# Modulation and first norm in one stage, and the mixing product begun inside the recurrence

## The reference

```
# first block, start
mod = silu(c) @ w_ada + b_ada                       # w_ada 1024 x 6144
sh_m, sc_m, g_m, sh_f, sc_f, g_f = split(mod, 6)
h = rms_norm(x, norm_mix) * (1 + sc_m) + sh_m
y = fox_mixer(h, ...)                               # begins with h @ w_in (q, k, v and 16 forget gates)
...
# second block
pool_out = multiscale_pool(...)
rwkv_out = rwkv7_mix(...)                           # a recurrence over tokens, 12 heads of 64
mixed = concatenate([pool_out, rwkv_out]) @ w_out   # 1024 x 1024
h = layer_norm(DEEPNORM_ALPHA * x + mixed, ln1_g, ln1_b)
ffn = hierarchical_moe(h, ...)                      # router logits, two of 32 experts per token
```

## Time and profile before

| | |
|---|---|
| median of 3 runs | 3073.77 us (3071.57 to 3078.01) |
| time of the profiled execution | 3072.45 us |
| its span in the profile | 3070.6 us |
| TensorE busy | 2856.3 us, 93% of the span |
| VectorE, ScalarE, GpSimd busy | 50%, 24%, 9% |
| granted TensorE clock, mean | 0.984 of full |

### The profile page before, as it was taken

One profiled execution on the slowest core, in us unless ns is written; L12 is line 12 of the kernel. 1 busy time (PEld: TensorE's weight loads), 2 busy tenths in 40 slices (PEclk: granted clock), 3 DMA queues, 4 the chain that ended last, 5 costly groups with the idle time before them and its releaser, 6 DMA issues. The chain is left out here.

```text
span 3070.6 us, 52396 instructions
## 1 busy us (share of the span) xinstructions
PE 2856.3 (93%) x20752; PEld 1903.6 (62%) x20752; DVE 1535.7 (50%) x4101; ACT 724.2 (24%) x1655; POOL 261.9 (9%) x343
## 2 busy tenths in 40 slices
PE   3999989989999999999999999999999797999996
PEld 2787456664688545885445777777777554444442
DVE  4543056761455566655654566666666366011115
ACT  2211056551200000000003344343444200111111
POOL 0000011100000000000000222121222100101001
PEclk9999999999999999999999999999999897999998
DMA  5101023321023453224453000000000200999965
GB/s 202 47 28 55 0 98 103 110 78 41 28 83 110 153 176 123 93 106 154 169 187 132 17 11 25 3 25 25 2 25 3 101 35 21 347 350 357 350 249 192
DMA packets 103873, 338.88 MB, mean 110 GB/s; under 512 B 6864, under 2 KB 16592, under 8 KB 94560
## 3 DMA queue, kind: packets, MB, share of 16 engines
q1 hardware_dynamic: 95696, 306.35, 27.9%
q0 software_dynamic: 6912, 25.17, 2.2%
q10 hardware_dynamic: 1040, 4.19, 0.3%
HBM read 302.60 MB, written 33.10 MB: 109 GB/s over the span
## 5 line engine op out<-in xcount | busy, mean ns | idle before, releaser
L1840 PE MATMUL rwkv_ps<-all_main,pre_ws 128*128 128x256 f32 x1152 | 290.9, 389 | 0.0
L1183 PE MATMUL mlp_ps<-mlp_w2s,all_main 128*128 128x512 f32 x512 | 239.6, 592 | 0.0
L2761 PE MATMUL ex_pg<-all_main,ex_xT 128*128 128x512 f32 x512 | 225.5, 594 | 0.0
L1840 PEld LDWEIGHTS rwkv_ps<-all_main,pre_ws 128*128 128x128 f32 x1152 | 207.6, 190 | 28.9
L2207 DVE TENSOR_TENSOR all_tail<-rwkv_ps,all_tail 128x256 f32<-128x256 f32 x216 | 91.6, 424 | 191.4 <-PE rwkv_ps L1946 144.7
L1183 PE MATMUL mlp_ps<-all_main 128*128 128x512 f32 x384 | 183.2, 592 | 0.7 <-DVE all_main L1396 0.7
L2761 PEld LDWEIGHTS ex_pg<-all_main,ex_xT 128*128 128x128 f32 x512 | 97.6, 191 | 122.4 <-issue 122.4
L1183 PEld LDWEIGHTS mlp_ps<-mlp_w2s,all_main 128*128 128x128 f32 x512 | 96.6, 190 | 117.8 <-issue 105.4
L2151 POOL TENSOR_TENSOR all_tail<-all_tail,pre_cst 128x256 f32<-128x256 f32 x120 | 99.9, 847 | 472.9 <-DVE all_tail L2207 299.3
L2068 ACT COPY all_tail<-rwkv_ps 128x256 f32<-128x256 f32 (+1 forms) x216 | 83.0, 396 | 219.4 <-PE rwkv_ps L1937 184.2
L1183 PEld LDWEIGHTS mlp_ps<-all_main 128*128 128x128 f32 x384 | 72.7, 190 | 93.2 <-issue 69.4
(11 more groups left out here) (439 smaller groups left out, 5087.9 us busy)
## 6 DMA issues: line engine op xcount, KB each, us to landing
mlp_w2s<-in_w SPq DMA_DIRECT2D x64, 1024.0 KB, 4.9
all_main<-in_w_gu SPq DMA_DIRECT2D x32, 2048.0 KB, 9.8
all_early<-in_w SPq DMA_DIRECT2D x32, 1024.0 KB, 4.7
att_wa<-in_w_ada SPq DMA_DIRECT2D x32, 512.0 KB, 3.9
all_early<-in_w_d SPq DMA_DIRECT2D x16, 1024.0 KB, 11.7
all_main<-in_w_d SPq DMA_DIRECT2D x16, 1024.0 KB, 11.2
y_rows<-ex_y SPq DMA_DIRECT2D x32, 512.0 KB, 3.1
qkv_wq<-in_w_qkv SPq DMA_DIRECT2D x6, 2048.0 KB, 7.5
```

The source lines that it names most:

```text
L1183: last = nc.tensor.matmul(ps[:, PRODUCTS.index(name), :], lhsT=lhsT, rhs=rhs, start=j == 0, stop=j == FPAIRS - 1)
L1840: last = nc.tensor.matmul(ps[:, bank, 0:UT], lhsT=ws[:, n, k, :], rhs=xT[:, k, (col + NB) % S:(col + NB) % S + UT], start=(k == 0), stop=( ...
L2761: last = nc.tensor.matmul(pg[:, n % 2, :], lhsT=xT[:, n % 2, k, :], rhs=gu[n][:, k, :], start=(k == 0), stop=(k == KT - 1))
```

## The change

`stage_modulation` and `stage_norm` become one block, `stage_start`. SP issues all its loads without a wait: first `x` in two halves of 2 MB, then `w_ada` in eight pieces of 1 MB, each into a place of its own in `main`. ScalarE squares a half and also scales it (an ACTIVATE in place of VectorE's multiplication). VectorE's accumulator is cut in two parts of 1024 columns, and TensorE waits for each apart; VectorE's two small steps for the second token half stand behind k = 1 and k = 2 in its list. TensorE transposes seven rounds into seven banks before it sums the columns, and the other nine after. The sixteen rounds are taken alternately by ScalarE and VectorE.

In the second block the PSUM tensor is now opened ahead of both stages. The layer norm's rows are loaded at the end of the recurrence's SP list. TensorE computes token tile 0 of the mixing product inside `stage_rwkv`, eight matmuls ahead of its last `body` and eight behind it; in `stage_mix_route` it starts with tile 1 and has no wait for `c_in` until the first logits.

```diff
-def stage_modulation(nc, x, cols1, w_ada, xres, modc, cols, silu, ones):
...
+def stage_start(nc, x, cols1, w_ada, xres, main, modc, cols, silu, hT, ones, ident):
...
+        pt = s.ps("pt", [P, 7, NB])
...
+        acc = main[:, 0:2, 2 * D:3 * D]
...
+        def bank(r):
+            return r % 7
+
+        def wait_taken(eng, r):
+
+            eng.wait_ge(taken_v if r % 2 else taken_a, r // 2 + 1)
...
                 sp.dma_start(cols[:], cols1).then_inc(cols_in, 16)
-                for g in range(KT // 2):
-                    if g >= 2:
-                        sp.wait_ge(w_used, 2 * g - 2)
-                    sp.dma_start(wa[:, g % 2, :, :], w_ada[2 * g * P:(2 * g + 2) * P, 0:2 * D].rearrange("(k p) c -> p k c", p=P)
-                                 ).then_inc(w_in[g % 2], 16)
+                for half in range(2):
+                    sp.dma_start(xres[:, half_of(half), :], x[half * NB:(half + 1) * NB, :].rearrange("(t p) d -> p t d", p=P)
+                                 ).then_inc(x_in[half], 16)
+                for k in range(KT):
+                    sp.dma_start(main[:, k, 0:2 * D], w_ada[k * P:(k + 1) * P, 0:2 * D]).then_inc(w_in[k], 16)
 
             @block.scalar
             def _(act):
                 act.wait_ge(cols_in, 16)
                 nc.scalar.activation(work[:, 0, :], cols[:, 0:KT], ACT.Exp, scale=-1.0).then_inc(silu_exp, 1)
-                act.wait_ge(w_in[1], 16)
-                act.dma_start(xres[:], x.rearrange("(t p) d -> p t d", p=P)).then_inc(x_in, 16)
-                act.wait_ge(x_in, 16)
+                for half in range(2):
+                    act.wait_ge(x_in[half], 16)
+                    for t in range(half * HT, (half + 1) * HT):
+                        nc.scalar.activation(xn[:, t, :], xres[:, t, :], ACT.Square, accum_out=ss[:, t:t + 1]).then_inc(sq_done, 1)
+                    act.wait_ge(var_ok, half + 1)
+                    nc.scalar.activation(st[:, 1, half_of(half)], st[:, 0, half_of(half)], ACT.Sqrt).then_inc(root, 1)
+                    act.wait_ge(rstd_ok, half + 1)
+                    for t in range(half * HT, (half + 1) * HT):
+                        nc.scalar.activation(xn[:, t, :], xres[:, t, :], ACT.Identity, scale=st[:, 2, t:t + 1]).then_inc(xn_done, 1)
+                act.wait_ge(finished, 3)
+                for r in range(0, 2 * KT, 2):
+                    half, c = r // KT, r % KT
+                    act.wait_ge(turned, r + 1)
+                    nc.scalar.activation(hT[:, c, half * NB:(half + 1) * NB], pt[:, bank(r), :], ACT.Identity,
+                                         scale=modc[:, 0, 0, c:c + 1], bias=modc[:, 0, 1, c:c + 1]).then_inc(taken_a, 1)
+                act.wait_ge(taken_a, KT)
...
+                def variance(half):
+                    dve.wait_ge(sq_done, (half + 1) * HT)
+                    nc.vector.tensor_scalar(st[:, 0, half_of(half)], ss[:, half_of(half)], 1.0 / D, EPS, ALU.mult, ALU.add
+                                            ).then_inc(var_ok, 1)
+
+                def inverse_root(half):
+                    dve.wait_ge(root, half + 1)
+                    nc.vector.reciprocal(st[:, 2, half_of(half)], st[:, 1, half_of(half)]).then_inc(rstd_ok, 1)
+
+                def weigh(k, part):
+                    if part == 0:
+                        dve.wait_ge(w_in[k], 16)
+                    out, w = acc[:, part, :], main[:, k, part * D:(part + 1) * D]
+                    if k == 0:
+                        nc.vector.tensor_scalar(out, w, silu[:, 0:1], None, ALU.mult).then_inc(w_used, 1)
+                        return
+                    dve.wait_ge(w_used, 2 * k + part - 1)
+                    nc.vector.scalar_tensor_tensor(out=out, in0=w, scalar=silu[:, k:k + 1], in1=out,
+                                                   op0=ALU.mult, op1=ALU.add).then_inc(w_used, 1)
+
...
+                variance(0)
+                inverse_root(0)
                 for k in range(KT):
-                    g = k // 2
-                    dve.wait_ge(w_in[g % 2], 16 * (g // 2 + 1))
-                    if k == 0:
-                        nc.vector.tensor_scalar(acc[:], wa[:, 0, 0, :], silu[:, 0:1], None, ALU.mult).then_inc(w_used, 1)
-                    else:
-                        dve.wait_ge(w_used, k)
-                        nc.vector.scalar_tensor_tensor(out=acc[:], in0=wa[:, g % 2, k % 2, :], scalar=silu[:, k:k + 1],
-                                                       in1=acc[:], op0=ALU.mult, op1=ALU.add).then_inc(w_used, 1)
+                    for part in range(2):
+                        weigh(k, part)
+                    if k == 1:
+                        variance(1)
+                    if k == 2:
+                        inverse_root(1)
                 dve.wait_ge(mm_mod, 1)
                 modulation_columns(nc, dve, pmod, cols, 0, modc, finished)
+                for r in range(1, 2 * KT, 2):
+                    half, c = r // KT, r % KT
+                    dve.wait_ge(turned, r + 1)
+                    nc.vector.tensor_scalar(hT[:, c, half * NB:(half + 1) * NB], pt[:, bank(r), :], modc[:, 0, 0, c:c + 1],
+                                            modc[:, 0, 1, c:c + 1], ALU.mult, ALU.add).then_inc(taken_v, 1)
+                dve.wait_ge(taken_v, KT)
...
-def stage_norm(nc, tag, xres, hT, modc, ident):
...
+                def turn(r):
+                    half, c = r // KT, r % KT
+                    if r % KT == 0:
+                        pe.wait_ge(xn_done, (half + 1) * HT)
+                    if r >= 7:
+                        wait_taken(pe, r - 7)
+                    for j in range(HT):
+                        last = nc.tensor.transpose(pt[:, bank(r), j * P:(j + 1) * P], xn[:, half * HT + j, c * P:(c + 1) * P], ident[:])
+                    last.then_inc(turned, 1)
+
+                for r in range(7):
+                    turn(r)
+                for m in range(2 * KT):
+                    if m % KT == 0:
+                        pe.wait_ge(w_used, 2 * KT - 1 + m // KT)
+                    last = nc.tensor.matmul(pmod[:, m:m + 1], lhsT=acc[:, m // KT, (m % KT) * P:(m % KT + 1) * P],
+                                            rhs=ones[:, 0:1], start=True, stop=True)
+                last.then_inc(mm_mod, 1)
+                for r in range(7, 2 * KT):
+                    turn(r)
...
-def stage_rwkv(nc, main, tail, early, pre, w_rkv, lora_up, lora_in, w_mix, ident):
+def stage_rwkv(nc, ps, main, tail, early, pre, w_rkv, lora_up, ln_rows, lora_in, w_mix, ident):
...
-        def each_unit(eng, body):
+        def each_unit(eng, body, around_last=None):
 
 
             for q in range(-1, UNITS + 1):
                 last = q % WPAIRS == WPAIRS - 1
                 nxt = q + 1 < UNITS
+                if q == UNITS and around_last:
+                    around_last(0)
                 body(q, 0 if last else (q % WPAIRS + 1) * UT, (q + 1) // WPAIRS if last and nxt else None, q > 0, 0 <= q < UNITS, nxt)
+                if q == UNITS and around_last:
+                    around_last(1)
 
...
                 sp.wait_ge(mix_in, 32)
+                sp.wait_ge(pe_a.sem, pe_a.at(UNITS - 1, "g"))
+                for n in range(2):
+                    sp.dma_start(lora_in[:, n, :], ln_rows[n].partition_broadcast(P)).then_inc(rows_in, 16)
+                sp.wait_ge(rows_in, 32)
...
+                def mix_first(n):
+                    if n == 0:
+                        pe.wait_ge(mix_in, 32)
+                        wait(pe, act_w, UNITS - 1, "y1")
+                        wait(pe, dve_w, UNITS - 1, "st3")
+                        wait(pe, dve_y, (PAIRS - 1) * WPAIRS, "y_out")
+                    for k in range(KT):
+                        nc.tensor.matmul(ps[:, n, :], lhsT=mixT[:, k, 0:P], rhs=main[:, k, D + n * NB:D + (n + 1) * NB],
+                                         start=(k == 0), stop=(k == KT - 1)).then_inc(mixed_first, 1)
+
                 pe.wait_ge(cleared, 2)
-                each_unit(pe, body)
+                each_unit(pe, body, mix_first)
+                pe.wait_ge(mixed_first, 2 * KT)
 
             @block.scalar
...
-                for n in range(2):
-                    sp.dma_start(rows[:, n, :], ln_rows[n].partition_broadcast(P)).then_inc(r_in, 16)
                 sp.dma_start(wr[:], w_router).then_inc(c_in, 16)
...
-                pe.wait_ge(c_in, 48)
-                for t in range(TT):
+                pe.sem_inc(mm, 1)
+                for t in range(1, TT):
                     if t >= 2:
                         pe.wait_ge(mm_taken, t - 1)
                     mix(t, 0, range(KT))
                     mix(t, 1, range(0, 4))
-                    if t:
-                        turn(t - 1)
+                    turn(t - 1)
                     mix(t, 1, range(4, KT)).then_inc(mm, 1)
-                    if t:
-                        logits(t - 1)
+                    if t == 1:
+                        pe.wait_ge(c_in, 48)
```

(23 more changed lines are left out.)

130 lines of the change are left out of this document (38 added, 92 removed).

## The result

The changed kernel takes **3047.66 us** (median of 4 runs, 3043.41 to 3049.81) against 3075.69 for the kernel before on the same chip (4 runs, 3071.57 to 3078.01): a ratio of 0.9908, 95% interval 0.9896 to 0.9920. The forecast was 3046.0. The profiled executions lie 25.6 us apart, 3072.45 and 3046.82.

What follows compares the result with a forecast made beforehand. It took the first stage to be bound by a chain of weights, sums and norm, and the second boundary by TensorE. Gains of 11.8 and 16.0 made 27.8, so 3073.8 - 27.8 = 3046.0 us, range 3040 to 3055.

Steps and rivals of the forecast that it cites:

- rival (a): First stage: halves of `x` do not land first, so no gain there; 3060 us, chance 0.08.
- The new wait: First stage: VectorE stands about 2 us at the second variance, until ScalarE's squares of the second half end.
- The nine late rounds of transposes being hidden: End of first stage: TensorE's rounds, 0.5 us each, hide behind ScalarE's and VectorE's rounds, 0.76 us or more each.
- the faster column sum: First stage: column sum records might take less than 0.22 us; a variation of the forecast worth -1.5 us.
- Everything behind it moves along: After the first stage: its 11.8 us gain shifts all later work, the forget gates' wait for their load included.
- (b): Second boundary: the moved matmuls run at the lower clock throughout, leaving a gain of 3; 3059 us, chance 0.08.
- (c): Mixing stage: whole tiles at the lower clock, 14.1 us more each, make it slower; three give 3088; chance 0.03.
- (d): Whole kernel: the change does nothing measurable, only if both (a) and (b) held; chance 0.03.
- The clock's part: Second boundary: 2.6 us of the gain from the lower clock avoided, 16.7 for the tile against 14.1.
- the first stage's term: First stage: ends near 54.3 instead of 66.1 us, a gain of 11.8 us.
- The boundary's term: Second boundary, recurrence to mixing: tile 0's transposes come at 2451.5 instead of 2467.46, a gain of 16.0 us.

Runs made afterwards that it cites:

- run 5: Changed kernel with VectorE's variance and reciprocal for the second token half one weight tile later each: 3046.9 us, ratio 0.9907.
- run 6: Changed kernel plus ten spare matmuls on TensorE, paced by VectorE's weighted sums, before the column sums: 3042.71 us, ratio 0.9892.
- Run 1: Kernel before with only the changed first stage; recurrence and mixing as before: 3061.32 us, ratio 0.9963.
- run 3: Changed kernel with token tile 0 multiplied in the mixing stage again, the norm's rows still loaded early: 3053.28 us, ratio 0.9934.
- run 4: Changed kernel with the norm's rows loaded at the mixing stage's head again and TensorE waiting for the tables before tile 1: 3055.35 us, ratio 0.9946.
- run 2: Changed kernel with the first stage of before, modulation and norm as two blocks: 3056.16 us, ratio 0.9949.
- run 10: Changed kernel with second variance and reciprocal one weight tile later, ten spare matmuls before the column sums, five before the forget gates: 3040.53 us, ratio 0.9895.
- run 7: Changed kernel with weights loaded before `x`, variances behind the sums, column sums ahead of all transposes: 3048.97 us, ratio 0.9910.

## Why the prediction was right, and where it was off

**Loads and ScalarE.** `x` was there at 11.54 (11.7 forecast), the first weights at 19.13 (19.0), the first half scaled at 21.88 (22.0), the second variance free at 26.02 (26.3). The second half of `x` landed 12.4 us after its issue, at 16.6 (16.5), so rival (a) did not occur.

**VectorE.** The new wait was 1.94 us (about 2), the sums 1.20 apart (1.20), the column sums at 39.46 (39.9). Without the wait (run 5) the column sums began 1.6 us earlier.

**TensorE, the step that was off.** "The nine late rounds of transposes being hidden" did not hold. I took a round at 0.5 us from a row at the full clock; they ran at the lower level up to 53, a round took 0.85 there, and the rounds of the stage 8.3 us instead of 6.9. With the 0.4 us won ahead of them, the stage ended at 55.30, not 54.3, and the gain was 10.8, not 11.8. The prediction checked the clock at the boundary and not here. The kernel before had a nearer row, of the same transposes in the same stage:

```profile
55.47 9.81 PE L241 MATMUL norm_pt<-all_ident,norm_xn 128*128 128x128 f32 x64 [9.81 <-DVE norm_xn L219]
```

The transposes that start there up to 59.8 last 0.42 us each and those from 60.2 on 0.27, the same two durations as in the change's late rounds. It also called the faster column sum a bound of 1.5 us; run 6 measured 3.3.

**What moves along.** "Everything behind it moves along" was true of the waits, not of the clock. The forget gates, and the first DMA of attention, in the kernel before and in the changed one:

```profile
69.81 15.60 PE L341 MATMUL qkv_ps<-h_hT,qkv_wf 128*16 128x512 f32 x32 [4.54 <-DMA qkv_fb<-in_b_f]
391.79 0.80 SPq L631 DMA_DIRECT2D att_frow<-f_rows  x2
```

```profile
378.49 0.80 SPq L637 DMA_DIRECT2D att_frow<-f_rows  x2
```

The 10.7 us at the first DMA were 13.3 at attention: 1.7 from the gates (13.91 at 1.00 here, 15.60 and partly below it before) and 0.9 because they began 2.43 us behind that DMA instead of 3.30. Run 1, with the same first stage, lost there instead (9.9 at attention), so this part is scatter. At the end of the recurrence 9.2 us were left. In the four executions with this first stage (runs 1, 3, 4 and the change) TensorE ended the recurrence 8.6, 12.9, 11.0 and 9.2 us before the 2425.5 of the earlier trace rows, which is 1.3, 1.0, 1.8 and 4.1 less than they had at attention. In the change's profile the granted clock was 0.50 around 2398, before it was not. Such a fall between 2380 and 2410 stands in all ten profiles with a changed first stage and in neither of the two with the old one (before, run 2), so it does not look like scatter. What makes it fall there I have not tested.

**The boundary.** 16.2 us against 16.0. The tile's transposes stood behind the first eight matmuls, no wait for the counts was left, the clock stayed at 1.00, and VectorE was done with tile 0 at 2439.11, 2.9 ahead of TensorE's need (3.0 forecast). Rivals (b), (c) and (d) are out. Runs 3 and 4 put the loads at 8.1 and the moved matmuls at 7.1. In the prediction's terms the rows of the two kernels split the 16.2 so: 8.2 for the wait (8.89 to 0.73, the rest being the block's end), 2.6 for the clock (the 56 records up to the transposes took 26.9 us and now 24.4), and 5.5 for the idleness and the two transposes under the last normalisation. The first was forecast as 8.9, the second as 2.6. The clock's part needs both edits: run 3, without the wait, still pays 2.3 of it, and run 4, with the wait back, 1.4. The longest gap of TensorE was 0.73, where the prediction had 0.5.

**Sum.** 27.8 forecast; 25.6 between the profiled executions, 28.0 between the medians, 27.1 from the two halves alone. That forecast and medians meet within 0.2 is luck: the first stage's term was 1.0 too large, and what followed it scattered by more than that. The boundary's term was right in size and in mechanism.

Two small readings of the prediction were wrong and changed nothing. `in_counts` is the fifth of SP's loads, not the sixth. And four multiplications of 0.748 us within 2.74 start 0.08 closer than they last, not 0.06, which also makes 1.20.

## What to carry to other kernels

Ask of each operation which of its inputs comes last: here only scale and shift needed the modulation, and moving everything else ahead of it gave 11 us at equal work. When one wait is removed at a boundary, look at what the engine does in the stretch before it as well: two edits of 7 and 8 us were needed to make TensorE continuous. Take the duration of a hidden step from a row of the same stage, with the engine as idle or as lightly loaded as it will be then: the late rounds ran at the lower level even where TensorE had been at work right before the column sums (run 10). Follow a gain to the next stage's first matmuls, where the clock can give 2 us of it back, and profile the same stage more than once before a gain of 2 us is believed.

## What the runs showed of the hardware that was not expected

Column sums of one column each took 0.218 us a record (6.99 for the 32 records of sixteen matmuls) in the kernel before, in the change and in run 7, whether the granted clock in the windows read 0.50 (the change, 38 to 46 us) or 1.00. They took 0.117 (3.73 for 32) in run 6 and 0.129 (4.12) in run 10, where TensorE had been at work right before them. A window of run 7 at 1.00, with 16 records that touch it:

```profile
28.00:31.00 3.00, 3.00 (x16) 3.00 (x15) 0.84 (x1) 0.00 (x0) 0.00 (x0) 1.00 1.03 411
```

The transposes of the kernel before show the same: 0.42 us each and then 0.27, with 1.00 in every window from 55 to 66 us. So the granted clock in the windows does not tell the rate of TensorE's first work after 10 to 39 us of idleness at the start of the program; why it does not is open.
